# Gates of a routed layer: one comparison for four tokens on VectorE, the gate multiplied in on ScalarE, and the gathered rows' dot products and weighted sums moved earlier

## The reference, cut to what matters

```python
def block(hb):                                    # 128 tokens
    q = (hb @ w_q).reshape(T, PEER_HEADS, 2, PEER_HALF)
    s = jnp.einsum('thpc,hpnc->thpn', q, sub_keys)
    sub_s, sub_i = lax.top_k(s, K)                # K = 16, of 128 keys, twice per head
    cand = (sub_s[:, :, 0, :, None] + sub_s[:, :, 1, None, :]).reshape(T, PEER_HEADS, K * K)
    top_s, top_i = lax.top_k(cand, K)
    k1 = jnp.take_along_axis(sub_i[:, :, 0], top_i // K, axis=-1)
    k2 = jnp.take_along_axis(sub_i[:, :, 1], top_i % K, axis=-1)
    expert = k1 * PEER_N_KEYS + k2
    g = jax.nn.softmax(top_s.astype(jnp.float32), axis=-1).astype(hb.dtype)
    ue = expert_u[expert]
    act = jax.nn.gelu(jnp.einsum('td,thkd->thk', hb, ue), approximate=False) * g
    ve = expert_v[expert]
    return jnp.einsum('thk,thkd->td', act, ve)
```

## Time and profile before

| | |
|---|---|
| median of 3 runs | 3867.21 us (3866.64 to 3868.18) |
| profiled execution | 3873.01 us, span 3871.1 us |
| mean granted TensorE clock | 0.97 |
| busy share | TensorE 94%, VectorE 56%, ScalarE 37%, GpSimd 20% |
| HBM | 530 MB read, 61 MB written |

### The profile page before, as it was taken

The page is one execution under the profiler, slowest core; times in us unless marked ns, Lnnn a source line. Parts: engine busy times, 40 slices in busy tenths (PEclk is TensorE's granted clock), DMA queues, the critical chain, the costliest instruction groups (busy, mean ns, idle before and its releaser), DMA issues.

```text
span 3871.1 us, 53964 instructions
## 1 busy us (share of the span) xinstructions
PE 3620.1 (94%) x21015; PEld 3063.3 (79%) x21015; DVE 2161.4 (56%) x4547; ACT 1414.5 (37%) x2285; POOL 762.4 (20%) x645
## 2 busy tenths in 40 slices
PE   6999998989998997999997899999999879999997
PEld 4877886878898997999995458868888745687885
DVE  3353343498989657787884454275333254537443
ACT  3232323323444442333334453263112335526222
POOL 0000000006988873465530000000000000000000
PEclk8999999999999998999998999999999989999998
DMA  5223223467887889999992001101111211120232
GB/s 212 98 77 142 98 95 118 148 208 272 281 282 264 309 287 360 359 354 323 375 352 86 22 28 55 60 18 46 65 66 66 76 55 39 61 82 23 98 103 82
DMA packets 220555, 594.49 MB, mean 154 GB/s; under 512 B 17936, under 2 KB 101520, under 8 KB 215952
## 3 DMA queue, kind: packets, MB, share of 16 engines
q1 hardware_dynamic: 156592, 380.68, 28.8%
q0 software_dynamic: 36864, 134.23, 9.7%
q10 hardware_dynamic: 26848, 76.14, 5.2%
HBM read 530.16 MB, written 60.82 MB: 153 GB/s over the span
## 4 chain that ended last, share of the span: by engine, by line
PE 77%; DVE 11%; DMA 7%; issue 2%; ACT 2%; POOL 0%; ACTq 0%; DVEq 0%; SPq 0%
PE bank L742 60%; PE bank L941 7%; DMA WR<-in_vrows 3%; PE bank L1035 2%; PE bank L1021 2%; PE bank L908 2%; DVE WL L1509 2%; PE bank L766 1%; DMA gelu_by_expert<-geU 1%; PE bank L803 1%; DMA rows<-in_urows,rk 1%; DMA rows<-in_vrows,rk 1%; DMA WR<-in_weights 1%; DVE Rw L1770 1%; ACT WH L1126 0%
## 5 line engine op out<-in xcount | busy, mean ns | idle before, releaser
L1509 DVE TENSOR_TENSOR WL<-WR,WH 128x1024 fp32r<-128x1024 f32 x512 | 627.7, 1228 | 823.4 <-ACT WH L1126 764.9
L1126 ACT ACTIVATE WH<-WR 128x1024 fp32r<-128x1024 f32 x512 | 537.1, 1058 | 811.3 <-DMA WR<-in_weights 201.2
L742 PE MATMUL bank<-H2h,WH 128*128 128x512 f32 (+2 forms) x1624 | 578.5, 356 | 4.5 <-DVE H2l L1537 4.5
L742 PE MATMUL bank<-H2h,WL 128*128 128x512 f32 (+2 forms) x1624 | 573.4, 353 | 0.0
L742 PE MATMUL bank<-H2l,WH 128*128 128x512 f32 (+2 forms) x1624 | 572.9, 353 | 0.0
L742 PE MATMUL bank<-Hh,WH 128*128 128x384 f32 (+1 forms) x1440 | 526.8, 366 | 25.7 <-DVE WL L1509 25.6
L742 PE MATMUL bank<-Hh,WL 128*128 128x384 f32 (+1 forms) x1440 | 511.9, 355 | 0.0
L742 PE MATMUL bank<-Hl,WH 128*128 128x384 f32 (+1 forms) x1440 | 511.2, 355 | 0.0
L941 PE MATMUL bank<-ah,WH 128*128 128x384 f32 x1024 | 346.0, 338 | 31.2 <-issue 18.0
L673 POOL DMA_INDIRECT rows<-in_urows,rk x128 | 164.9, 1288 | 960.4 <-DVE rk L1795 740.9
L742 PEld LDWEIGHTS bank<-H2h,WH 128*128 128x128 f32 (+1 forms) x1624 | 307.1, 189 | 52.3 <-issue 7.7
(11 more groups left out here) (310 smaller groups left out, 5679.4 us busy)
## 6 DMA issues: line engine op xcount, KB each, us to landing
WR<-in_weights SPq DMA_DIRECT2D x498, 512.0 KB, 3.5
WR<-in_vrows SPq DMA_DIRECT2D x128, 512.0 KB, 9.4
gelu_by_expert<-geU ACTq DMA_DIRECT2D x128, 192.0 KB, 4.8
gates_by_expert<-tab ACTq DMA_DIRECT2D x24, 1024.0 KB, 6.3
geV<-gelu_by_expert SPq DMA_DIRECT2D x32, 768.0 KB, 12.0
Gt<-gates_by_expert SPq DMA_DIRECT2D x16, 1536.0 KB, 18.4
x_kept<-X ACTq DMA_DIRECT2D x2, 3072.0 KB, 8.7
X<-x_kept ACTq DMA_DIRECT2D x2, 3072.0 KB, 11.0
```

What stands on the lines that cost most here:

```text
L742: yield nc.tensor.matmul(b[0:rows, out_cols], a, r, start=n == 0, stop=n == len(pairs) - 1)
L1126: act.activation(WH[:, n % SLOTS, :, :].rearrange("p a b -> p (a b)"), WR[:, c % SLOTS, :, :].rearrange("p a b -> p (a b)"), ACT.Copy)\
L1509: v.tensor_tensor(WL[:, n % SLOTS, :, :].rearrange("p a b -> p (a b)"), WR[:, plan.splits[n] % SLOTS, :, :].rearrange("p a b -> p (a b)"), ...
```

## The change

Three things change. `hots` makes one comparison of 128x512 (with `iota128` and the keys of four tokens repeated by address) in place of four comparisons with a multiplication. A new function `hot_weights` on ScalarE multiplies the four gates in, in place, after a wait for that comparison (`hot_keys`). And the two schedules move: the dots begin at b = 14 and are all done in the up phase, and the weighted sums begin at chunk 4 of the down phase.

```diff
 def dots_by(b):
-    return 15 * max(0, min(b, NK) - 18) // 16 + 2 * max(0, b - NK)
+    return min(PICKS, 9 * max(0, b - 13) // 8)
 def sums_by(c):
-    return PICKS * max(0, c - 14) // (NK - 15)
+    return PICKS * max(0, c - 3) // (NK - 4)
...
+            def hot_weights(tt, q):
+                n = tt * (P // 4) + q
+                act.wait_ge(hot_keys, n + 1)
+                for t in range(4):
+                    c = 4 * q + t
+                    hot = hotA[:, n % HOTS, t, :]
+                    act.activation(hot, hot, ACT.Copy, scale=KT[:, tt % 2, 2, c:c + 1]).then_inc(hot_a, k.inc(hot_a))
...
                 out_of(("U", b), geU[:, b % 2, :], slice(0, TN), ACT.Gelu)
+                if hot_in(b):
+                    hot_weights(*hot_in(b))
                 if hot_in(b - HOT_LAG):
                     gates_out(*hot_in(b - HOT_LAG))
...
-                if c == 13:
+                if c == 1:
                     act.wait_ge(dots_done, 1)
                     act.activation(dots, dots, ACT.Gelu).then_inc(dots_gelu, 1)
...
-                for t in range(4):
-                    c = 4 * q + t
-                    v.tensor_scalar(hotA[:, n % HOTS, t, :], consts["iota128"][:, :],
-                                    KT[:, tt % 2, 0, c:c + 1], KT[:, tt % 2, 2, c:c + 1],
-                                    ALU.is_equal, ALU.mult).then_inc(hot_a, k.inc(hot_a))
+                v.tensor_tensor(hotA[:, n % HOTS, :, :], consts["iota128"][:, :].unsqueeze(1).to_broadcast([P, 4, P]),
+                                KT[:, tt % 2, 0, 4 * q:4 * q + 4].unsqueeze(2).to_broadcast([P, 4, P]),
+                                ALU.is_equal).then_inc(hot_keys, k.inc(hot_keys))
...
+            while dotted < PICKS:
+                dot(dotted)
+                dotted += 1
+            dve.wait_ge(row_used, PICKS)
+            v.engine_nop().then_inc(dots_done, 1)
...
-                while dotted < min(PICKS, dots_by(NK + c)):
-                    dot(dotted)
-                    dotted += 1
-                    if dotted == PICKS:
-                        dve.wait_ge(row_used, PICKS)
-                        v.engine_nop().then_inc(dots_done, 1)
-                if c == 14:
+                if c == 2:
                     dve.wait_ge(dots_gelu, 1)
```

More of the change, by code:

```diff
@@ L494, in build @@
         kt_ready = sem("kt_ready")
-        hot_a, hot_b = sem("hot_a"), sem("hot_b")
+        hot_keys, hot_a, hot_b = sem("hot_keys"), sem("hot_a"), sem("hot_b")
         a_ready = sem("a_ready")
@@ L1913, in _ @@
                     summed += 1
-            assert summed == PICKS and dotted == PICKS
+            assert summed == PICKS
             split[0] = S["V", NK - 1] + 1
```

## The result

The changed kernel takes 3886.93 us (median of 13 runs, 3879.12 to 3892.45) against 3869.43 us (13 runs of the kernel before beside it): ratio 1.0040, 95% interval 1.0030 to 1.0049. It is slower by 17.5 us, a little over half of the forecast +31 us. Its profiled span is 3884.3 us, 13.2 more than before.

A forecast was written before the change was run, and what follows sets the result against it. VectorE was taken to bound the front, TensorE the groups, TensorE and DMA the down phase. Terms 7 + 33 - 9 = +31 us gave a median of 3898 us, range 3852 to 3935 us.

The forecast's parts named there:

- The front: 808 to 881 us, before the first dense gates: six more dots on full VectorE delay TensorE, +7 us.
- The ring: Groups of four tokens: `WH`, `WL`, comparison, multiplications and `tab` copy wait in a 5.02 us round; +47 us before deductions.
- the 1.5 us per four chunks: Groups: `geU` store waits, double dots and long steps falling on a ring without room; bounds 0 and 2.2 us.
- What was taken off: Groups: 5 us for `WL`'s lead and 9 us, half the waits at b = 53 and 85, off the +47.
- Term 2: Groups of four tokens, 881 to 1434 us: ring cost less deductions, 47 - 5 - 9 = +33 us.
- Rival B: Groups: GpSimd becomes the bound, blocked by each new comparison plus extra dots and gathers; +49 us, total 3914 us, chance 0.15.
- The down phase: 1487 to 2033 us: 26 rows (13.6 MB) leave and sums spread over 124 chunks, recovering stalls behind `al`; -9 us.

The follow-up runs named there:

- the grid above: Time of the groups: changed kernel 617.8 us; one of four `hotB` left out 621.6; multiplications one chunk later 608.9; both edits 592.6.
- the relieved kernel: Changed kernel with GpSimd leaving out one of four `hotB` from the fifth group on (every fourth token's gates wrong): 3884.04 us, ratio 1.0042.
- the last pair of kernels that compute the right thing: Changed kernel with four single-input comparisons and multiplications one chunk later: 3866.71 us; the same with dots from b = 21: 3864.01 us.

## Why the prediction was right, and where its numbers were off

**The front, +7**: measured +7.3. It stays with the old comparisons (141.5 us) and vanishes when no new dot lies ahead of b = 21 (134.1).

**The ring**: the mechanism, its members and its round of 5.02 us were right, and all its priced parts (1.20 us forecast and 1.19 measured, 0.70 and 0.69). Opening it (the multiplications one chunk later) and lengthening it (four comparisons) move the time as a ring must. What was too large in the sum is the 1.5 us per four chunks for the waits for `geU` stores and other disturbances. The median of four chunks from b = 23 on is 22.36 us against the forecast 23.15 (21.21 before), that is 0.7 instead of 1.5 over 21.65. The store waits fell from 51.9 to 10.0 us instead of falling on the ring: ScalarE comes later to the wait for a store that was issued two chunks earlier, and so mostly finds it landed (worked out from the order of its stream; no run separates it). I had read a row of waiting as a cost that moves along, where it was slack that the delay uses up. 24 x (22.36 - 21.2) = +28 us in place of +47. Nor is this all the ring's: without the ring, the dots and gathers alone cost 9 of the 23.7 us.

**What was taken off**: of the 9 us at b = 53 and 85 little came; the three waits at L917 went from 20.1 to 18.8 us. The long rounds are in chunks 21 to 85 (+21.1 us); from 85 on, where VectorE has less to choose, four chunks take 21.2 to 21.9 us in most cases, and it is +2.6. Net the term is +23.7 us, where +33 was forecast.

**GpSimd**: "about 0.3 us a group [...] no stall" had the cost right and the consequence wrong. `hotB` went from 915 to 1020 ns, 4 x 0.105 = 0.42 us a group with the extra dots, 0.37 of them by the comparison alone (1008 ns), and GpSimd had no room to take it: 20.2 us of TensorE's waits. I had compared 5.1 us of work with 5.3 of pace as averages, but gathers, long VectorE steps and the dots come in bunches, and `hotB` leads the product by two chunks at most. Term 2 likewise put the 18 extra dots and gathers at nothing ("That helps nobody directly"), and they cost 9 us in the groups. Rival B's mechanism is thus there, at a third of its size, beside the ring and not in its place; as the grid above shows, without it the ring alone would have cost as much. Where TensorE waits in the profile after (at `hotB`) therefore does not tell what sets the pace: that took the relieved kernel.

The Trainium skill, "SBUF — State Buffer", section "SBUF: two separate sides", has GpSimd, where it reads SBUF, fully blocked for the whole of a VectorE instruction with two SBUF inputs, if that one started first. Between the kernels with the ring opened, which differ in the form of the comparison alone, GpSimd's 384 `hotB` differ by 0.088 us each, 34 us, or 0.35 us for each comparison of 0.69. That is the direction of the rule and half of its size at the hardest: not each comparison meets a `hotB` from its start.

The trace before shows the same by neighbours, with each `hotB` sorted by the VectorE instruction that ran longest beside it. With none beside it, `hotB` takes 605 ns in the mean. Beside the old `hotA` comparisons, which read one SBUF tile and single columns, it takes 627; beside a dot 1203, and beside `WL` 1398, and these two read two tiles. So the four old comparisons left GpSimd free, as the forecast had assumed, while `WL` and the dots already held it up.

**The down phase**: -9 was forecast, -19.8 came. The step that failed is "The stalls are 13.0 us, and that is the most that can come back". All 13 came back, and 6.6 us more out of TensorE's busy time (541.7 to 535.1 us for the same matmuls): delays too short to be called stalls there. By eighths, the first two lost 7.7 us (the 26 dots at two a chunk) and the fourth to sixth 11.9 (the sums at 128 in 113 chunks, at DMA share 0.99). With the old pace of the sums the first part came back and the second did not: 547.6 us. So the even spread gives about 12 us and the moved dots 7 to 8.

**The sum** over the profile: +7.3 + 23.7 - 19.8, -0.5 and -0.9 in the rest, and +3.5 of spread, is the +13.2 us of the span; the medians differ by 17.5. The sign hung on luck in part. The terms that were forecast and priced, the front, the new comparison (14 to 15 us) and the down phase, add up to about +2 us by the profiles; the other 9 are those of the dots and gathers in the groups, which the forecast had at nothing. Both misses, 9 us too much for the groups and 11 too little for the down phase, had the same sign.

**Open**: why the groups take 5 us more with the dots from b = 21 in the last pair of kernels that compute the right thing, while 6 us of front come back. More gathers fall into fewer chunks (`hotB` 954 ns against 925), but no kernel separates their issue on GpSimd from VectorE's dots.

## What to carry to other kernels

Work that is moved to an idle engine is free only if it doesn't stand, on both engines, between what each waits for from the other: follow one round and add it up, and if it closes near the pace of the bound engine, put the moved work one round later. Two late engines need not add up, so relieving the one that the bound engine visibly waits for may give nothing until the other is relieved too. And a stall in the trace counts what it would cost to be late only after its slack is taken off.

## What was not expected of the hardware

GpSimd's comparison of 128x128, the same instruction throughout, took 823, 915, 925, 1013 or 1020 ns in the mean of a kernel, and 605 to 1398 ns in one trace by what VectorE ran beside it; spans on GpSimd are rough. And a wait for two engines can carry neither's name: the 3.03 us ahead of the product at 1060.38 us are called "issue", while GpSimd's `hotB` ended 0.1 us before.
